# Layer 0's modulation, split between the preamble's TensorE and VectorE inside the latent-attention heads

## The chip, the cores and the metric

The kernel runs on one NeuronCore of a Trainium2 chip. The metric is the device time of one execution in microseconds (us); the median of the runs is compared.

## The reference, cut to what matters

One step of a four-layer trunk over 128 context and 512 latent tokens, model width D = 1024, float32. Each layer is

```python
mod = (jax.nn.silu(cond) @ w_mod[l] + b_mod[l]).reshape(cond.shape[0], 6, D_MODEL)[:, :, None, :]
h = rmsnorm(x, g_norm1[l]) * (1.0 + mod[:, 1]) + mod[:, 0]
out, ctx_tensors = token_mixer(l, h, ctx)
x = x + mod[:, 2] * out
h = rmsnorm(x, g_norm2[l]) * (1.0 + mod[:, 4]) + mod[:, 3]
x = x + mod[:, 5] * swiglu(h, w_ffn_in[l], w_ffn_out[l])
```

`cond` is one vector for the context tokens and another for the latent ones, so the modulation of a layer is a product of two rows of 1024 with a matrix of 1024 x 6144 (24 MB): six kinds of 1024 values, for two conditions. Kinds 0 and 1 (shift and scale) are used at the start of a layer, kind 2 after its token mixer, kinds 3 to 5 in its feed-forward part. The token mixer of layer 0 is latent attention with 8 heads.

## The kernel before, in words

The activations lie transposed in SBUF, 128 channels to a tile, 640 tokens to a row. Every large product is made of float32r multiplies of a high and a low part: a weight panel is fetched into `raw`, split into `w_hi` and `w_lo`, and TensorE multiplies three combinations (L310). The five engines have a program each, joined by semaphores; the order on each is written out by hand.

**Preamble.** The input is turned into tiles by TensorE (L829) and copied by ScalarE (L1342, L1343). VectorE sums the squares (L1862, L1864). Small vectors are turned into `vecs`, from which ScalarE makes `silu_c`, the 2 x 1024 activated conditions. Then `first_modulation` works out all six kinds of layer 0's modulation: 12 chunks of 512 columns, each fetched in one DMA of 2 MB (L649, L654) and multiplied by 8 TensorE multiplies with `silu_c` as the two-column weight (L761). ScalarE copies each two-row result (L1374) and TensorE turns it into columns, four small multiplies a chunk (L768). VectorE adds the bias (L1932). Only then come the first norm (column sums L326, the factor on ScalarE, `scaled` on VectorE L2009, the modulation of each tile on ScalarE L1389 and L1392, the low part L2014) and the projection into the latent ranks (`mla_in`, 6 panels).

**Layers 1 to 3** have their modulation worked out on VectorE, inside the previous layer's feed-forward part: a tile of `w_mod` is multiplied by a column of `silu_c` and added to an accumulator (L1971, L1973), and TensorE turns and VectorE sums the accumulators.

**A latent-attention head.** While TensorE multiplies for head h, it prepares head n = h + 1. Its order is: `gqn(n)`, scores 2, turned 0, `gqr(n)`, `ssqn(n)`, scores 3, `ssqr(n)`, `gkn(n)`, turned 1, `rotqr(n)`, scores 4, `sskn(n)`, `gv(n)`, turned 2 to 4, scores 0 and 1 of head n, `turned_v(n)` among them, and last the output product `pe_output` (L373). Here "scores t" is a query tile against all keys (L354) and "turned t" the transposition of its probabilities (L365). VectorE's order is: maximum 2, probabilities 2, maximum 3, `q_nope`, `q_rope` (L451), `q_roped` (L455, L456, L458), maximum 4, probabilities 3, `k_nope`, probabilities 4, then maxima 0 and 1 of head n, probabilities 0, `split_head` (L467 to L472), probabilities 1. ScalarE makes the exponentials (L388), the norm factors (L412, L414) and the copies. GpSimd splits the panels of the heads (L731 `w_hi`, L734 `w_lo`), one pair of operations when `gqr` is done and one when `gv` is done. The queue SP fetches each head's two panels as soon as `raw` is free; behind the last head's panels stand those of the output projection `wo0`, which ScalarE and VectorE split (`first_low_parts`). The last head prepares nothing and is shorter.

Of the kernel before, what the change touches and what calls it, by code (L numbers as in the profile page):

```python
# [18 lines left out]
ALU = mybir.AluOpType  # L19
# [3 lines left out]
P = 128  # L23
D = 1024
# [149 lines left out]
def build(nc, a):  # L174
# [3 lines left out]
    with ExitStack() as ctx:  # L178
# [57 lines left out]
        mod_ready = sem("mod_ready")  # L236
        mod_turned = sem("mod_turned")
        mod_summed = sem("mod_summed")
        scratch_free = sem("scratch_free")
# [19 lines left out]
        PRE = [Steps(pre_pe, ["x0", "x1", "x2", "x3", "x4", "x5", "x6", "x7", "vecs", "bmod", "lam"]),  # L259
               Steps(pre_act, ["vecs", "silu", "lamexp", "sp"]),  # L260
               Steps(pre_dve, ["ready", "lamsum", "lamdiff", "lamall", "bmod", "splog"])]
# [290 lines left out]
        first_mod_w = [work[:, k * KT * 512:(k + 1) * KT * 512] for k in (2, 1, 0)]  # L552
        first_mod_rows = work[0:2, WORK - 2 * 512:WORK].rearrange("p (b n) -> p b n", b=2)
# [26 lines left out]
        def _(sp):  # L580
# [64 lines left out]
            w = a["w_mod"][0].rearrange("(k p) n -> p k n", p=P)  # L645
            for b in range(3):
                if b == 1:
                    sp.wait_ge(scratch_free, 1)
                sp.dma_start(first_mod_w[b].rearrange("p (k n) -> p k n", k=KT),  # L649
                             w[:, :, b * 512:(b + 1) * 512]).then_inc(first_mod_in[b], 16)  # L650
            with sp.Fori(1, 4) as i:
                for b in range(3):
                    sp.wait_ge(first_mod_used, i * 3 + (b + 1 - 3))
                    sp.dma_start(first_mod_w[b].rearrange("p (k n) -> p k n", k=KT),  # L654
                                 w[:, :, bass.ds(i * 1536 + b * 512, 512)]).then_inc(first_mod_in[b], 16)

            for layer in range(DEPTH):
                if layer == 0:
                    win = a["mla_w_in"][0].rearrange("(k p) n -> p k n", p=P)
# [3 lines left out]
                    ph = phases["mla_in"]  # L663
                    for t in range(6):
                        c0 = t * P if t < 5 else 576
                        if t >= 2:
                            sp.wait_ge(split_done, t - 1)
                        sp.dma_start(raw[t % 2][:, :].rearrange("p (k n) -> p k n", k=KT),
                                     win[:, :, c0:c0 + P]).then_inc(raw_in[t % 2], 16)
                    panels("mla", lambda i, j: uq[:, :, bass.ds(i * 192, 192)] if j == 0  # L670
                           else ukv[:, :, bass.ds(i * 256, 256)])
# [81 lines left out]
        def _(pe):  # L753
            def first_modulation():

                with pe.Fori(0, 2) as i:
                    for q in range(7):
                        if q < 6:
                            pe.wait_ge(first_mod_in[q % 3], i * 32 + (16 * (q // 3) + 16))
                            for kt in range(KT):  # L760
                                last = nc.tensor.matmul(psum[q % 2][0:2, 0, :], silu_c[:, kt * 2:kt * 2 + 2],  # L761
                                                        first_mod_w[q % 3][:, kt * 512:(kt + 1) * 512],
                                                        start=(kt == 0), stop=(kt == KT - 1))
                            last.then_inc(first_mod_used, 1)
                        if q:
                            pe.wait_ge(first_mod_row, i * 6 + q)
                            for k in range(4):
                                last = nc.tensor.matmul(psC[:, 1, bass.ds(i * 48 + ((q - 1) * 4 + k) * 2, 2)],  # L768
                                                        first_mod_rows[:, (q - 1) % 2, k * P:(k + 1) * P],
                                                        ident[0:2, 0:2], start=True, stop=True)  # L770
                            last.then_inc(first_mod_turned, 1)
# [18 lines left out]
            LRU_PE.open(pe)  # L790

            def norm(n):
                if n == 0:
                    pe.wait_ge(mod_ready, 1)
                pe.wait_ge(square_done, (n + 1) * KT)
                sum_rows(psC, ones, [square_sum if n else square_sum0], TH).then_inc(sums_done, 1)
# [25 lines left out]
            pe.wait_ge(const_in, 16)  # L822
# [9 lines left out]
            pe.wait_ge(const_in, 16 * 22)  # L832
            for k in range(2):
                last = nc.tensor.transpose(psC[:, 0, k * P:(k + 1) * P], vec_rows[k], ident)
            pes.mark(last, "vecs")
            nc.tensor.transpose(psD[:, 0, 0:P], vec_rows[2], ident)
            pes.mark(nc.tensor.transpose(psD[:, 0, P:2 * P], vec_rows[3], ident), "bmod")
            dves.wait(pe, "lamdiff")
            pes.mark(nc.tensor.matmul(psC[:, 1, 0:1], ones[0:1, :], lam_tmp[0:1, 4:5], start=True, stop=True), "lam")
            acts.wait(pe, "silu")  # L840
            dves.wait(pe, "bmod")
            dves.wait(pe, "lamall")
# [3 lines left out]
            for layer in range(DEPTH):  # L846
# [6 lines left out]
                if layer == 0:  # L853
# [93 lines left out]
                    def head(h, more):  # L947
# [372 lines left out]
        def _(act):  # L1320
# [17 lines left out]
            act.dma_start(tables[:, :], a["tables"]).then_inc(tables_in, 16)  # L1338
# [13 lines left out]
            act.sem_inc(first_mod_turned, 2)  # L1352
            pes.wait(act, "vecs")
            act.sem_inc(silu_done, 1)
# [4 lines left out]
            acts.mark(nc.scalar.activation(sc[:, :, 1], vecs[:, VEC["c"]:VEC["c"] + KT], ACT.Silu), "silu")  # L1359
            dves.wait(act, "lamsum")  # L1360
            acts.mark(nc.scalar.activation(lam_tmp[0:1, 2:4], lam_tmp[0:1, 0:2], ACT.Exp), "lamexp")

# [4 lines left out]


            with act.Fori(0, 6) as i:
                for b in range(2):  # L1370
                    act.wait_ge(first_mod_used, i * 2 + (b + 1))

                    act.wait_ge(first_mod_turned, i * 2 + (b + 1))
                    nc.scalar.activation(first_mod_rows[:, b, :], psum[b][0:2, 0, :],  # L1374
                                         ACT.Copy).then_inc(first_mod_row, 1)
# [1070 lines left out]
```

## Time and profile before

| | us |
|---|---|
| median of 3 runs (3607.37 to 3613.88) | 3607.74 |
| the profiled execution | 3609.12 |
| its span, first to last instruction | 3606.8 |
| TensorE busy in the span | 3318.1 (92%) |
| VectorE busy | 1878.0 (52%) |
| ScalarE busy | 1132.7 (31%) |
| GpSimd busy | 117.5 (3%) |

The span is what the profiler saw between the first and the last instruction; 2.3 us of the execution lie around it. PE is TensorE's multiplying part, PEld its loading of weights, DVE VectorE, ACT ScalarE, POOL GpSimd, SP the queue that issues most DMAs. A share of busy time is an average over stages that differ; the mean granted TensorE clock of the whole span is 0.963 of full speed.

### The profile page before, as it was taken

The numbers are of one execution on the slowest core, as the hardware profiler recorded it, in microseconds if no ns is written. First come the engines' busy times: TensorE is split into PE (matmuls) and PEld (weight loads), VectorE is DVE, ScalarE is ACT, GpSimd is POOL, SyncE is SP. The second block draws the span as 40 slices with busy tenths as digits, with TensorE's granted clock in tenths as the row PEclk, the third lists the DMA queues.
The fourth block names the chain that finished last, engine by engine and source line by source line (L and its number), as shares of the span: only waits on it lengthen the run. The fifth ranks groups of instructions, "written<-read, shape, count | busy, mean of one in ns | idle before, by whom it ended". The sixth has DMA issues, their size and how long they took to land.

```text
span 3606.8 us, 52935 instructions
## 1 busy us (share of the span) xinstructions
PE 3318.1 (92%) x20320; PEld 3011.4 (83%) x20320; DVE 1878.0 (52%) x2728; ACT 1132.7 (31%) x1742; POOL 117.5 (3%) x72
## 2 busy tenths in 40 slices
PE   7979898999998998899999788989999897899999
PEld 2556677999987776789999766779999897899999
DVE  2133346858354666466763544567573688533333
ACT  1334433211125555232111333232111377321111
POOL 0311100000000000000000221000000000000000
PEclk9989999999999999899999899999999999999999
DMA  7300013444221110153532210143432221222222
GB/s 260 109 21 13 18 33 120 145 146 142 74 82 37 42 47 17 47 176 120 177 93 70 57 31 18 35 145 124 162 123 76 62 67 47 59 76 76 76 74 77
DMA packets 421861, 304.11 MB, mean 84 GB/s; under 512 B 12019, under 2 KB 389494, under 8 KB 421622
## 3 DMA queue, kind: packets, MB, share of 16 engines
q1 hardware_dynamic: 411412, 293.23, 26.2%
q10 hardware_dynamic: 10338, 9.41, 0.8%
q8 instruction: 69, 1.13, 0.1%
q14 instruction: 42, 0.34, 0.0%
HBM read 298.49 MB, written 4.10 MB: 84 GB/s over the span
## 4 chain that ended last, share of the span: by engine, by line
PE 83%; DVE 7%; ACT 5%; DVEq 2%; issue 2%; ACTq 1%; DMA 1%; SPq 0%
PE psB L310 29%; PE psA L310 29%; PE psD L310 7%; PE psC L373 3%; PE psA L354 2%; PE psC L326 2%; PE psC L365 2%; PE psB L354 2%; ACT h_hi L1392 1%; PE psA L761 1%; ACT work L1389 1%; PE psB L761 1%; ACTq L1391 1%; ACT work L412 1%; DMA raw<-in_w_ffn_in 1%
## 5 line engine op out<-in xcount | busy, mean ns | idle before, releaser
L1410 ACT ACTIVATE w_hi<-raw 128x1024 fp32r<-128x1024 f32 (+1 forms) x309 | 319.3, 1035 | 1165.2 <-PE psB L310 766.2
L1943 DVE TENSOR_TENSOR w_lo<-raw,w_hi 128x1024 fp32r<-128x1024 f32 (+1 forms) x309 | 367.9, 1192 | 347.8 <-ACT w_hi L1410 347.5
L310 PE MATMUL psA<-h_hi,w_hi 128*128 128x320 f32 x1616 | 384.5, 320 | 72.0 <-DVE h_lo L2014 59.9
L310 PE MATMUL psB<-h_hi,w_hi 128*128 128x320 f32 x1616 | 370.0, 310 | 15.5 <-DVE w_lo L2296 15.5
L310 PE MATMUL psA<-h_lo,w_hi 128*128 128x320 f32 x1616 | 375.4, 314 | 0.0
L310 PE MATMUL psA<-h_hi,w_lo 128*128 128x320 f32 x1616 | 375.1, 314 | 0.0
L310 PE MATMUL psB<-h_lo,w_hi 128*128 128x320 f32 x1616 | 369.2, 310 | 0.0
L310 PE MATMUL psB<-h_hi,w_lo 128*128 128x320 f32 x1616 | 369.1, 310 | 0.0
L310 PEld LDWEIGHTS psA<-h_hi,w_hi 128*128 128x128 f32 x1616 | 273.9, 192 | 91.9 <-issue 43.8
L1973 DVE SCALAR_TENSOR_TENSOR work<-work,silu_c 128x1024 f32<-128x1024 f32 x252 | 312.5, 1281 | 12.4 <-issue 0.9
L310 PEld LDWEIGHTS psB<-h_hi,w_hi 128*128 128x128 f32 x1616 | 271.0, 188 | 17.1 <-DVE w_lo L2296 17.1
L310 PEld LDWEIGHTS psA<-h_lo,w_hi 128*128 128x128 f32 x1616 | 277.2, 192 | 0.0
L310 PEld LDWEIGHTS psA<-h_hi,w_lo 128*128 128x128 f32 x1616 | 276.8, 192 | 0.0
L310 PEld LDWEIGHTS psB<-h_lo,w_hi 128*128 128x128 f32 x1616 | 271.3, 188 | 0.0
L310 PEld LDWEIGHTS psB<-h_hi,w_lo 128*128 128x128 f32 x1616 | 271.1, 188 | 0.0
L310 PE MATMUL psA<-act_hi,w_hi 128*128 128x320 f32 x960 | 221.5, 312 | 16.0 <-DVE w_lo L1943 14.9
L310 PE MATMUL psA<-act_lo,w_hi 128*128 128x320 f32 x960 | 220.3, 311 | 0.0
L310 PE MATMUL psA<-act_hi,w_lo 128*128 128x320 f32 x960 | 220.0, 311 | 0.0
L310 PE MATMUL psB<-act_hi,w_hi 128*128 128x320 f32 x960 | 218.8, 309 | 0.0
L310 PE MATMUL psB<-act_hi,w_lo 128*128 128x320 f32 x960 | 218.7, 309 | 0.0
L310 PE MATMUL psB<-act_lo,w_hi 128*128 128x320 f32 x960 | 218.7, 309 | 0.0
L310 PE MATMUL psD<-h_hi,w_hi 128*128 128x320 f32 (+1 forms) x672 | 182.0, 353 | 17.5 <-DVE h_lo L2014 8.6
(290 smaller groups left out, 5137.8 us busy)
## 6 DMA issues: line engine op xcount, KB each, us to landing
raw<-in_w_ffn_in SPq DMA_DIRECT2D x176, 512.0 KB, 3.9
work<-in_w_mod SPq DMA_DIRECT2D x144, 512.0 KB, 4.8
raw<-in_w_ffn_out SPq DMA_DIRECT2D x64, 512.0 KB, 3.9
work<-in_w_mod SPq DMA_DIRECT2D x12, 2048.0 KB, 7.9
raw<-in_w_ffn_out SPq DMA_DIRECT2D x32, 384.0 KB, 3.3
raw<-in_diff_w_in SPq DMA_DIRECT2D x24, 512.0 KB, 3.8
raw<-in_lru_w_in SPq DMA_DIRECT2D x16, 512.0 KB, 4.0
raw<-in_gqa_w_in SPq DMA_DIRECT2D x12, 512.0 KB, 3.8
```

The source lines that it names most:

```text
L310: last = nc.tensor.matmul(out[:, b, 0:half], w[slot][:, kt * cols + c0:kt * cols + c0 + P], r[:, o:o + half], start=(kt == 0 and p == 0), ...
L326: last = nc.tensor.matmul(out[:, b, 0:half], ones_, sq[:, b * half:(b + 1) * half], start=(k == 0), stop=(k == len(pieces) - 1))
L354: last = nc.tensor.matmul(s[:, b, 0:n], q[:, q0:q0 + P], k[:, k0:k0 + n], start=(m == 0), stop=(m == len(pairs[c]) - 1))
L365: last = nc.tensor.transpose(psC[:, k // 4, (k % 4) * P:(k % 4 + 1) * P], probs[(h.k % 2 * QT + t) % 2][0][:, k * P:(k + 1) * P], ident)
L373: nc.tensor.matmul(psC[:, 0, 0:NLAT], V[:, (k + 1) * P:(k + 2) * P], PT[:, k * NLAT:(k + 1) * NLAT], start=(k == 0), stop=(k == 4))
L412: nc.scalar.activation(halves(out, half), ps[:, :, 0:half], ACT.Ln, bias=eps, scale=1.0 / count)
L761: last = nc.tensor.matmul(psum[q % 2][0:2, 0, :], silu_c[:, kt * 2:kt * 2 + 2], first_mod_w[q % 3][:, kt * 512:(kt + 1) * 512], start=(kt ...
L1389: nc.scalar.activation(s_, s_, ACT.Identity, bias=mod_col(layer, 3 * which, kt, cond), scale=gains[:, cond * KT + kt:cond * KT + kt + 1])
L1391: act.drain()
L1410: nc.scalar.activation(w_hi[s][:, 0:n], raw[s][:, 0:n], ACT.Copy).then_inc(hi_done, 1)
L1943: nc.vector.tensor_tensor(w_lo[s_][:, 0:n], raw[s_][:, 0:n], w_hi[s_][:, 0:n].bitcast(F32), ALU.subtract).then_inc(split_done, 1)
L1973: last = nc.vector.scalar_tensor_tensor(acc[cond], w_, c_, acc[cond], ALU.mult, ALU.add)
```

## The change

- In the preamble `first_modulation` works out kinds 0 and 1 alone. It goes by tiles of 128 rows and 2048 columns (8 DMAs of 1 MB, three buffers), 4 multiplies a tile into two banks each of psA and psB: 32 multiplies in place of 96. Then come 2 copies on ScalarE and 16 turns on TensorE, in one go, in place of 12 copies and 48 turns in between. The first two `mla_in` panels are fetched behind the fourth and fifth tile.
- `silu_c` is made ahead of the copies of the input; the column sums of the first norm, its factor and `scaled` are made while the multiplies run; the small vectors of the last layer (`late_vectors`) are worked out behind the first norm.
- Kinds 2 to 5 (16 MB) are worked out in the 8 heads, 512 columns a head: 8 DMAs of 256 KB into two halves of `raw[2]`, 16 products on VectorE in four groups of 4 (`late(0)` to `late(3)`), into two accumulators that lie in the second half of `tables`, and 8 TensorE multiplies with one column of ones (`late_mod_turn`), behind turned 4.
- The second half of `tables` is fetched after the last head's `late_mod_turn`, in front of the panels of `wo0` on SP.

The diff, cut to its core:

```diff
             for kt in range(KT):
+                if kt >= 3:
+                    sp.wait_ge(first_mod_used, kt - 2)
+                sp.dma_start(first_mod_w[kt % 3], a["w_mod"][0][kt * P:(kt + 1) * P, 0:2 * D]).then_inc(first_mod_in[kt % 3], 16)
+                if kt in (3, 4):
+                    mla_in_panel(kt - 3)
...
+                    def late_mod(i, k):
+                        for kt in range(KT):
+                            sp.wait_ge(late_mod_used, i * (2 * KT) + (k * KT + kt + 1))
+                            sp.dma_start(late_mod_w[kt % 2], a["w_mod"][0][kt * P:(kt + 1) * P, bass.ds(i * D + (2 * D + k * 512), 512)]
+                                         ).then_inc(late_mod_in[kt % 2], 16)
...
+                    for k in range(2):
+                        late_mod(HEADS // 2 - 1, k)
+                    sp.wait_ge(late_mod_turned, HEADS + 1)
+                    sp.dma_start(tables[:, 2 * NLAT:4 * NLAT], a["tables"][:, 2 * NLAT:4 * NLAT]).then_inc(tables_in, 16)
...
+                for kt in range(KT):
+                    pe.wait_ge(first_mod_in[kt % 3], 16 * (kt // 3 + 1))
+                    for q in range(4):
+                        last = nc.tensor.matmul(psum[q // 2][0:2, q % 2, :], silu_c[:, kt * 2:kt * 2 + 2],
+                                                first_mod_w[kt % 3][:, q * 512:(q + 1) * 512],
+                                                start=(kt == 0), stop=(kt == KT - 1))
+                    last.then_inc(first_mod_used, 1)
...
+            def late_mod_turn(h):
+
+                pe.wait_ge(late_mod_used, h.at(KT, KT + 2))
+                for t in range(4):
+                    for cond in range(2):
+                        last = nc.tensor.matmul(psC[:, 1, bass.ds(h.at(8, late_at + t * 2 + cond), 1)],
+                                                late_mod_acc[cond][:, t * P:(t + 1) * P], ones[:, 0:1],
+                                                start=True, stop=True)
+                last.then_inc(late_mod_turned, 1)
...
                         pe_turned(pe, A, h, 4, m_probs)
+                        late_mod_turn(h)
                         if more:
...
+            def late_mod_product(h, n):
+
+                kt, cond = n // 2, n % 2
+                if cond == 0:
+                    if kt:
+                        dve.drain()
+                    dve.wait_ge(late_mod_in[kt % 2], h.at(64, 16 * (kt // 2 + 1)))
+                    if kt == 0:
+                        dve.wait_ge(late_mod_turned, h.at(1, 1))
+                w_, c_ = late_mod_w[kt % 2], silu_c[:, kt * 2 + cond:kt * 2 + cond + 1]
+                if kt == 0:
+                    last = nc.vector.tensor_scalar(late_mod_acc[cond], w_, c_, None, ALU.mult)
+                else:
+                    last = nc.vector.scalar_tensor_tensor(late_mod_acc[cond], w_, c_, late_mod_acc[cond], ALU.mult, ALU.add)
+                if cond:
+                    last.then_inc(late_mod_used, 1)
...
                         largest(h, 2)
                         probs(h, 2)
+                        late(0)
                         largest(h, 3)
                         prep(q_nope)
                         prep(q_rope)
+                        late(1)
                         prep(q_roped)
                         largest(h, 4)
                         probs(h, 3)
+                        late(2)
                         prep(k_nope)
                         probs(h, 4)
+                        late(3)
```

Three places where the order of instructions changes. First VectorE inside a head, from the probabilities of tile 2 (TENSOR_SCALAR 128x640) to `q_rope`. Before:

```order
L442 TENSOR_SCALAR work<-work 128x640
L95 REGISTER_ALU
L426 TENSOR_REDUCE work<-psB 128x1 [waits mla_att_pe]
L430 TENSOR_SCALAR work<-work 128x1
L95 ISA
L451 SCALAR_TENSOR_TENSOR work<-work,vecs 128x640 [waits mla_prep_act]
L95 REGISTER_ALU
L451 SCALAR_TENSOR_TENSOR work<-work,vecs 128x640 [waits mla_prep_act]
L95 ISA
L455 TENSOR_TENSOR work<-psC,tables 128x512 [waits mla_prep_pe]
```

And now, from the same TENSOR_SCALAR to `q_nope`:

```order
L444 TENSOR_SCALAR work<-work 128x640
L1991 ISA
L1993 ISA [waits late_mod_in0]
L1996 TENSOR_SCALAR tables<-raw,silu_c 128x512 [waits late_mod_turned]
L1996 TENSOR_SCALAR tables<-raw,silu_c 128x512
L1998 SCALAR_TENSOR_TENSOR tables<-raw,silu_c,tables 128x512 [waits late_mod_in1]
L1998 SCALAR_TENSOR_TENSOR tables<-raw,silu_c,tables 128x512
L95 REGISTER_ALU
L428 TENSOR_REDUCE work<-psB 128x1 [waits mla_att_pe]
L432 TENSOR_SCALAR work<-work 128x1
L95 ISA
L453 SCALAR_TENSOR_TENSOR work<-work,vecs 128x640 [waits mla_prep_act]
```

The four products of `late(0)` stand between the probabilities and the next maximum (TENSOR_REDUCE); the line numbers of the helpers are two higher. The other three groups stand in the same way ahead of `q_roped`, of `k_nope` and of the next head's first maximum.

Second TensorE at the end of a head, from turned 4 to the next head's scores 0. Before:

```order
L365 MATMUL psC<-consts,work 128x128 [waits mla_att_act,mla_att_dve]
L95 REGISTER_ALU
L354 MATMUL psB<-work 128x320 [waits mla_att_act,mla_prep_dve]
L354 MATMUL psB<-work 128x320 x3
L95 REGISTER_ALU [waits mla_att_act]
L934 MATMUL psC<-consts,work 128x128 [waits mla_prep_act]
L934 MATMUL psC<-consts,work 128x128 x5
```

And now, with the first and the last of the eight turns:

```order
L367 MATMUL psC<-consts,work 128x128 [waits mla_att_act,mla_att_dve]
L815 ISA [waits late_mod_used]
L815 MATMUL psC<-consts,tables 128x1
L815 ISA
...
L815 ISA
L815 MATMUL psC<-consts,tables 128x1
L95 REGISTER_ALU
L356 MATMUL psB<-work 128x320 [waits mla_att_act,mla_prep_dve]
L356 MATMUL psB<-work 128x320 x3
```

Eight multiplies of one column, behind a wait for VectorE's last product of the head, have come in between turned 4 and scores 0.

Third the queue SP from the heads to `wo0`. Before, the loop over the heads' panels and the first panel of `wo0` behind it:

```order
L595 ISA [waits split_done]
L595 DMA raw<-in_mla_w_uq 128x3x192
L594 REGISTER_ALU
L595 ISA [waits split_done]
L595 DMA raw<-in_mla_w_ukv 128x2x256
L607 REGISTER_ALU
L607 COMPARE_AND_BRANCH
L607 UNCONDITIONAL_BRANCH
L607 ISA
L595 ISA [waits split_done]
L595 DMA raw<-in_mla_w_o 128x8x128
```

And now, from the last two heads' tiles of `w_mod` on:

```order
L686 DMA raw<-in_w_mod 128x512 [waits late_mod_used] x16
L706 DMA tables<-in_tables 128x1024 [waits late_mod_turned]
L615 UNCONDITIONAL_BRANCH
L615 ISA
L603 ISA [waits split_done]
L603 DMA raw<-in_mla_w_o 128x8x128
```

The panels of `wo0` now stand behind a wait for the last head's turn and behind a fetch of 512 KB.

## Rows read from the trace of the kernel before

**Rows 1.** Stretches: us, busy PE, PEld, DVE, ACT, POOL; PEclk, DMA share, GB/s.

```profile
30.00:128.00 98.00, 97.39 (x288) 27.11 (x288) 4.77 (x31) 8.33 (x13) 8.43 (x4) 0.97 0.74 257
353.97:391.30 37.33, 32.90 (x152) 24.79 (x151) 13.93 (x31) 17.28 (x34) 4.87 (x4) 0.95 0.05 15
```

**Rows 2.** Chain of waits, preamble: start us, us, engine, tile, line, count.

```profile
30.48 9.47 PE psA L761 x16
39.95 6.87 PE psB L761 x16
46.82 0.98 PE psC L768 x8
...
127.92 0.33 DVE mods L1932 x2
...
132.16 0.49 ACT work L1389
```

**Rows 3.** Timeline of the start: start us, us, engine, line, operation [idle before].

```profile
12.49 0.60 ACT L1342 ACTIVATE x<-psA 128x512 f32<-128x512 f32 x1 [1.65 <-PE psA L829]
...
19.47 0.38 ACT L1355 ACTIVATE vecs<-psC 128x256 f32<-128x256 f32 x1
...
21.54 1.28 ACT L1361 ACT_TABLE_LOAD   x1
```

**Rows 4.** DMA issues of the first 200 us: count, KB each, us to landing.

```profile
work<-in_w_mod SPq DMA_DIRECT2D x12, 2048.0 KB, 7.9
raw<-in_mla_w_in SPq DMA_DIRECT2D x6, 512.0 KB, 3.9
...
raw<-in_mla_w_ukv SPq DMA_DIRECT2D x2, 256.0 KB, 2.7
```

**Rows 5.** Instructions that read silu_c: ns min/median/max, first and last start.

```profile
L1973 DVE SCALAR_TENSOR_TENSOR work<-work,silu_c x252: 1275/1282/1287, 609.8 to 2679.2; 128x1024 f32<-128x1024 f32 x126
```

**Rows 6.** Timeline of one head, 353.9 to 391.4 us.

```profile
355.82 0.55 DVE L442 TENSOR_SCALAR work<-work 128x640 f32<-128x640 f32 x1
...
356.69 1.15 POOL L731 TENSOR_TENSOR w_hi<-raw,consts 128x576 fp32r<-128x576 f32 x1 [15.47 <-PE psD L310]
...
359.87 0.82 DVE L426 TENSOR_REDUCE work<-psA 128x1 f32<-128x640 f32 x1 [3.50 <-PE psA L354]
...
362.58 0.89 DVE L451 SCALAR_TENSOR_TENSOR work<-work,vecs 128x640 f32<-128x640 f32 x1 [0.82 <-ACT work L414]
...
365.61 0.69 DVE L455 TENSOR_TENSOR work<-psC,tables 128x512 f32<-128x512 f32 x1 [2.15 <-PE psC L916]
...
367.72 1.56 PE L326 MATMUL psC<-work,consts 128*128 128x384 f32 x4 [1.70 <-DVE work L458]
...
373.53 0.29 DVE L442 TENSOR_SCALAR work<-work 128x128 f32<-128x128 f32 x1
...
375.68 0.41 PE L365 MATMUL psC<-consts,work 128*128 128x128 f32 x1
...
375.96 1.04 POOL L731 TENSOR_TENSOR w_hi<-raw,consts 128x512 fp32r<-128x512 f32 x1 [16.63 <-PE psD L310]
```

**Rows 7.** Timeline of VectorE beside GpSimd, 2010 to 2026 us.

```profile
2009.89 0.82 DVE L1862 TENSOR_TENSOR work<-x 128x640 f32 x1
...
2015.02 1.39 DVE L1862 TENSOR_TENSOR work<-x 128x640 f32<-128x640 f32 x1
...
2015.81 2.88 POOL L734 TENSOR_TENSOR w_lo<-raw,w_hi 128x1024 fp32r<-128x1024 f32 x1
...
2016.49 2.88 DVE L1864 TENSOR_TENSOR work<-work 128x640 f32<-128x640 f32 x1
```

**Rows 8.** Chain of waits at the end of the last head.

```profile
501.08 0.55 DVE work L442
...
506.83 6.06 PE psC L373 x10
...
513.10 7.04 PE psA L310 x48
```

More of the change, by code:

```diff
@@ L550, in build @@
         mod_acc = [[c(MUNIT) for _ in range(2)] for _ in range(2)]
-        first_mod_w = [work[:, k * KT * 512:(k + 1) * KT * 512] for k in (2, 1, 0)]
-        first_mod_rows = work[0:2, WORK - 2 * 512:WORK].rearrange("p (b n) -> p b n", b=2)
+        first_at = QT * D + 1024 + T
+        first_mod_w = [work[:, first_at + k * 2 * D:first_at + (k + 1) * 2 * D] for k in range(3)]
+        first_mod_rows = work[0:2, first_at:first_at + 2 * D]
+        first_rms = tables[:, 2 * NLAT:2 * NLAT + T]
+        late_mod_w = raw[2][:, 0:512], raw[2][:, 512:1024]
+        late_mod_acc = tables[:, 2 * NLAT:3 * NLAT], tables[:, 3 * NLAT:4 * NLAT]
+        late_at = 512 - 4 * 2 * KT
+        assert first_at + 6 * D <= WORK
         c = Carve()
@@ L662, in _ @@
                     wo = a["mla_w_o"][0]
[L663 to L671, printed above, removed]
+                    ph = phases["mla"]
@@ L754, in first_modulation @@
             def first_modulation():
[L756 to L771, printed above, removed]
+                for kt in range(KT):
+                    pe.wait_ge(first_mod_in[kt % 3], 16 * (kt // 3 + 1))
[4 more added lines that the diff above has]
+                    last.then_inc(first_mod_used, 1)
+                    if kt == 4:
+                        pe.wait_ge(square_done, KT)
+                        PRE[2].wait(pe, "lamdiff")
+                        sum_rows(psD, ones, [square_sum0], TH).then_inc(sums_done, 1)
+                        PRE[0].mark(nc.tensor.matmul(psC[:, 1, 0:1], ones[0:1, :], lam_tmp[0:1, 4:5], start=True, stop=True),
+                                    "lam")
@@ new lines, in first_modulation @@
+                pe.wait_ge(first_mod_row, 1)
+                for k in range(2 * KT):
+                    last = nc.tensor.matmul(psC[:, 0, 2 * k:2 * k + 2], first_mod_rows[:, k * P:(k + 1) * P],
+                                            ident[0:2, 0:2], start=True, stop=True)
+                last.then_inc(first_mod_turned, 1)
+            def late_mod_turn(h):
[6 more added lines that the diff above has]
+                last.then_inc(late_mod_turned, 1)
@@ L820, in _ @@
             pes, acts, dves = PRE
-            pe.wait_ge(const_in, 16)
+            pe.wait_ge(const_in, 16 * 22)
+            for k in range(2):
+                last = nc.tensor.transpose(psC[:, 0, k * P:(k + 1) * P], vec_rows[k], ident)
+            pes.mark(last, "vecs")
+            nc.tensor.transpose(psD[:, 0, 0:P], vec_rows[2], ident)
+            pes.mark(nc.tensor.transpose(psD[:, 0, P:2 * P], vec_rows[3], ident), "bmod")
             pe.wait_ge(x_in, 32)
@@ L831, in _ @@
                 pes.mark(last, f"x{kt}")
[L832 to L839, printed above, removed]
             acts.wait(pe, "silu")
-            dves.wait(pe, "bmod")
-            dves.wait(pe, "lamall")
             pe.wait_ge(x_done, KT)
@@ L1907, in _, with late_vectors @@
+            dve.drain()
+            def late_vectors():
+                dve.wait_ge(tables_in, 16)
+                acts.wait(dve, "sp")
+                ys, s_, s2, acc, tmp = (lru_small[:, 80 + 16 * k:96 + 16 * k] for k in range(5))
+                nc.vector.tensor_scalar(tmp, ys, 2.0, None, ALU.add)
                 dve.drain()
-                nc.vector.tensor_scalar(acc, acc, 1.0 / k, None, ALU.add)
+                nc.vector.reciprocal(tmp, tmp)
                 dve.drain()
-            nc.vector.tensor_tensor(acc, acc, s_, ALU.mult)
```

189 lines of the change are left out of this document (113 added, 76 removed).

## Prediction

> **What bounds the kernel now.** I read the table of stretches first. In the preamble TensorE is busy for 97.39 of 98.00 us, and with the modulation alone; a head takes 37.33 us, 32.90 of them TensorE's, while VectorE works 13.93 [rows 1]. The chain of waits says the same of the preamble: from 30.48 us it runs through L761 and L768 without a gap, until VectorE adds the bias at 127.92 and ScalarE modulates the first tile at 132.16 [rows 2]. What is taken from L761 there comes off the time one for one. A head is different. Its timeline shows a relay [rows 6]: TensorE turns, VectorE makes `q_roped`, TensorE's sums at 367.72 are released by VectorE after 1.70 us of waiting. VectorE has room on average, but a product in the wrong place lands on that relay. Last comes the end of the last head, where TensorE goes from L373 straight into `wo0` at 513.10 [rows 8].
>
> **Preamble: what goes.** Behind the landing of the small vectors, now turned first (about 11.7 us), ScalarE runs from the copy of `vecs` to the end of the second table load. Before, that was 19.47 to 22.82, so 3.35 us, and the eight input copies took 12.49 to 19.47, so 7.0 us [rows 3]. With 0.2 for the exponential that makes 11.7 + 3.4 + 0.2 + 7.0 = 22.3; 0.7 more as TensorE turns the tiles with idle time in between: 23.0. Eight multiplies took 6.87 us, the first eight 9.47 [rows 2]. So 32 take 27.5, and I add 1.3, half of the slow start (ends 0 and 2.6). The column sums of the norm, now among them, cost 1.1 by their columns, the small lambda multiply 0.3: end at 53.2. Then one after the other: two copies of 2 x 1024 by ScalarE, some 2.2 (estimate: a copy of 1024 columns, twice); 16 turns at 0.98 us for 4, so 3.9, and 0.8 for a TensorE that has just been idle (ends 0 and 3); VectorE's bias 0.33, gains and a flag, 1.1 in all. Sum 61.2, and 0.5 for hand-overs: ScalarE's first tile at 61.7 in place of 132.16, a gain of **70.4 us**, ends 66 and 73. Squares, column sums and `scaled` fit beside the multiplies: VectorE is done with them by about 52. The small vectors of the last layer, 31 operations of some 0.2 us, go behind the norm, where VectorE waits for the six panels anyway. DMA: 8 MB in 8 fetches, three of them issued from 9.5 us, when TensorE starts at 23; 2 MB landed after 7.9 us, 0.5 MB after 3.9 [rows 4], so 1 MB in about 5, and a buffer has 2 x 3.4 us. No wait, even with two panels in between.
>
> **A head with preparation (seven).** One product of 512 columns: the form of 1024 takes 1.28 us [rows 5], a two-input operation of 512 takes 0.69 (L455) [rows 6]; I take 0.74, a pair 1.4, a group of four 2.9, `late(0)` 2.4 as its first two have one tensor input.
> - `late(0)` starts at 356.4, behind the TENSOR_SCALAR of 355.82, and must be done by 359.87: hidden.
> - `late(1)` starts where `q_rope` ends, 363.5, and ends at 366.5; `q_roped` started at 365.61. **0.9 us** on the relay. TensorE's sums, and what hangs on them, come 0.9 later.
> - `late(2)` stands ahead of `k_nope`, which ends at 374.1; scores 0, which wait for it, were not due before 376. Hidden. Probabilities 4 then end at 374.8 (373.82 before), 0.9 later like the rest.
> - `late(3)` ends at 377.8. TensorE has done turned 4, at 376.1 + 0.9 = 377.0. It stands for **0.8 us**, and behind it on TensorE stand scores 0, `turned_v`, scores 1 and the output product.
> - 8 turns: L768 does 4 multiplies with as many loads in 0.98 us, so **2.1 us** with the hand-over.
> - The 64 fetches of 256 KB: one is issued when the product two tiles earlier is done and lands 2.7 us later [rows 4]. Tile 4 is asked for at 365.0, needed at 370.1; tile 6 at 371.6, needed at 374.9. They fit, the last by 0.6 us. On SP each head's panels stand ahead of its tiles and were waiting in `raw` before; nobody waits for them.
>
> That is 3.8 us, the floor, with two things to add that the trace of before shows in other places. Beside GpSimd a VectorE operation of two SBUF inputs and 640 columns, 0.82 us alone, took 1.39 and 2.88 [rows 7]. The second ends at 2019.37, 0.68 behind GpSimd's end at 2018.69: the two take turns. In a head GpSimd splits at 356.69 (2.6 us with its low part) and 375.96 [rows 6], inside `late(0)` and `late(3)`. If they take turns, `late(0)` ends near 361.2 and pushes `q_rope` by 0.6, `late(3)` by 1.1: 1.5 together, in the six heads with a split. I take 1.0, since a pair may pass without a break.
>
> Those rows bear out the Trainium skill, SBUF — State Buffer, section "SBUF: two separate sides": VectorE operations of two SBUF inputs and GpSimd operations exclude each other for a whole instruction. By that rule to the letter the heads cost 3 us more than with my 1.0 (6 x 0.5); without it, 6 us less. The trace agrees, in this one place.
>
> The other is the clock. A head's granted clock is 0.95 [rows 1], which is 3.7 us at half speed of 37.3, around 373.5 to 377 where TensorE waits between turns. The new stand and the one-column turns come right behind. More time at 1.2 GHz would fall on scores 0 and `turned_v`: I take 1.2 us a head, ends 0 and 3.
>
> So 3.8 + 1.0 + 1.2 = 6.0 for six heads and 5.0 for the seventh: **41.0 us**, ends 26.6 and 56.
>
> **The last head** has no other work to hide in. Its products and their fetches form a chain, since a tile lands 2.8 us after the product two tiles back. Probabilities 2 end at 501.6 [rows 8]; tiles 0 and 1 are done at 502.6 and 504.1; tiles 2 and 3 land at 505.4 and 506.9, done 506.8 and 508.4; maximum 4 and probabilities 3 take 1.4; tiles 4 and 5 land at 509.6 and 511.2, done 511.2 and 512.7; tiles 6 and 7 land at 514.0 and 515.5, the last is done at 517.0. The turns end at 519.1, and the output product starts there in place of 506.83 [rows 8]: 12.3 us. Then `wo0`: SP issues 512 KB of tables and two panels only at 519.1; the first panel lands near 524.4, ScalarE and VectorE split it in 2.4: TensorE starts at 526.8 in place of 513.10. **13.7 us**, and 0.8 for the clock: 14.5, ends 12 and 17.
>
> **Sum.** -70.4 + 41.0 + 14.5 = -14.9. On the profiled execution's 3609.1 that gives 3594.2. It lies 1.4 above the median of the runs, so 3592.8 on the median; I put down **3593**. A difference of 0.2% is 7.2 us, about what a measurement can tell.
>
> **Rivals.**
> - *Cheap heads.* GpSimd and VectorE pass each other and the clock stays: heads 27, last head 13.7, so -70.4 + 40.3 = -30.1: 3578. For it: VectorE would still be busy only 25 of 41 us. Against: rows 7. Chance 0.17.
> - *The tiles land late.* The last tile of a group has 0.6 us to spare. If a fetch takes 3.9 as one of 512 KB does, `late(3)` ends 0.6 to 1.2 later in each of seven heads and the last head's chain grows by 3: +9 us, 3602, no change that can be told. Also here: a preamble bound by its landings (+5). Chance 0.16.
> - *Half clock (slower).* Place: TensorE between turned 4 and the output product. It stands, loads weights for single columns, and is granted 1.2 GHz for turns, scores 0, `turned_v` and scores 1, 7.1 us of work at full speed with the turns; less what was slow already (0.6), some 6 us a head in place of 1.2. Seven heads: +34 us, 3626. For it: the clock fell at smaller gaps (0.95). Against: scores are dense work, behind which it rose each time. It decides from 7.9 us a head on ((70.4 - 14.5) / 7); slower by 0.2% needs 9.0. Chance 0.13.
> - *The change doesn't do what it says:* the preamble stays bound by something else, such as the copies of the input; the timeline leaves nothing that long. Chance 0.02, at 3600 or more.
>
> **How the numbers follow.** My forecast has 0.52, from 3584 to 3600. Faster by over 0.2% (under 3600.5): nearly all of that, the cheap heads, and little of the late tiles: 0.69. Same: part of the late tiles and the milder half of the slow clock: 0.19. Slower: 0.12. The range leaves out the ends of the cheap heads and the upper half of the slow clock: 3574 to 3616.
>
> **What would show it.** L761 with 32 multiplies ending near 53 us and the first L1389 near 62. A head of 43.3 us, of which TensorE waits about 1 to 2 behind VectorE's last product; `q_roped` released by the products, not by TensorE; VectorE products of over 1 us beside GpSimd; L815 at some 2 us a head. `wo0` starting 14 us after its old distance from the last head's first score, released by a DMA. I am wrong if a head takes under 41 or over 45 us, if tiles of `w_mod` release VectorE in the middle heads, or if the first norm comes after 66.

## The result, and the profile after

The changed kernel takes **3624.07 us** (median of 5 runs, 3618.60 to 3629.20); the kernel before 3607.74. The ratio is **1.0046**, 95% interval 1.0032 to 1.0059: slower, by 16 us, where 15 us less were forecast. The profiled execution took 3624.07 us, its span is 3621.7 us (before 3606.8). The page's first lines, of after:

```profile
PE 3302.8 (91%) x20256; PEld 3032.7 (84%) x20256; DVE 1991.5 (55%) x2858; ACT 1125.7 (31%) x1731; POOL 121.6 (3%) x72
...
PEclk9888889999998999999999899999999999999999
```

**The preamble did what was forecast.** Its chain of waits (start, us, what):

```profile
26.21 1.88 PE psA L794 x4
28.09 1.72 PE psB L794 x4
...
53.80 1.73 PE psB L794 x4
...
57.52 4.38 PE psC L806 x32
...
62.76 0.49 ACT work L1434
```

The multiplies end at 55.53 us, the turns at 61.9, ScalarE's first tile of the norm starts at 62.76; before, it was 132.16 [rows 2]. That is 69.4 us gained.

**The heads gave it all back.** The stretch of one regular head of after (the columns are those of [rows 1]):

```profile
314.80:362.55 47.75, 39.66 (x167) 29.80 (x167) 27.89 (x47) 17.27 (x34) 5.62 (x4) 0.86 0.18 56
```

A head takes 47.75 us, before 37.33 [rows 1]; the granted clock in it fell from 0.95 to 0.86. TensorE is *busier* (39.66 for 32.90) although only eight one-column multiplies came in: the same work lasts longer. The timeline shows where. L1998 is VectorE's late products, L815 the turns, L356 the scores, L766 and L769 GpSimd's splits of a panel, L328 the column sums, L977 `turned_v`:

```profile
329.40 2.31 PE L328 MATMUL psC<-work,consts 128*128 128x384 f32 x4 [2.53 <-DVE work L460]
...
330.94 2.92 DVE L1998 SCALAR_TENSOR_TENSOR tables<-raw,silu_c,tables 128x512 f32<-128x512 f32 x4 [0.16 <-issue]
...
336.41 4.53 DVE L1998 SCALAR_TENSOR_TENSOR tables<-raw,silu_c,tables 128x512 f32<-128x512 f32 x4 [0.17 <-issue]
...
337.30 1.42 POOL L766 TENSOR_TENSOR w_hi<-raw,consts 128x512 fp32r<-128x512 f32 x1 [17.09 <-PE psD L312]
...
338.80 1.59 POOL L769 TENSOR_TENSOR w_lo<-raw,w_hi 128x512 fp32r<-128x512 f32 x1
...
341.08 3.57 PE L815 MATMUL psC<-consts,tables 128*128 128x1 f32 x16 [3.68 <-DVE tables L1998]
344.51 4.62 PE L356 MATMUL psA<-work 128*128 128x320 f32 x8
348.92 1.49 PE L977 MATMUL psC<-consts,work 128*128 128x128 f32 x6
```

Read it from the back. Scores of 8 multiplies take 4.62 us here; the same form takes 2.32 in the dense parts of the head. The turns take 3.57. Ahead of them TensorE stood for 3.68 us, released by VectorE's last group of four products, which took 4.53 us in place of the 2.92 of the group before it: GpSimd's two splits lie inside it. The table of stretches has the granted clock: half (1.2 GHz) from 341.5 to 350, full (2.4 GHz) before TensorE stood:

```profile
335.00:337.00 2.00, 1.61 (x11) 1.00 0.67 176
341.50:350.00 8.50, 8.50 (x29) 0.50 0.28 93
```

From the last head's column sums (L328, 472.68) to the first multiply of `wo0` (529.69) it takes 57.0 us; before, 33.25 (479.61 to 512.86; the chain takes `wo0` up a little later [rows 8]). 7.9 of these 23.8 us lie ahead of the seventh head's output product. The chain of waits shows the other 15.9: tiles of `w_mod` that land one by one, the turns at half clock, and only then the fetch of `wo0`'s first panel:

```profile
513.46 2.53 DMA raw<-in_w_mod
...
516.03 1.43 DVE tables L1998 x2
...
517.50 3.59 PE psC L815 x16
...
521.77 5.38 DMA raw<-in_mla_w_o
...
527.17 1.06 ACT w_hi L1455
...
528.33 1.24 DVE w_lo L2007
...
529.69 1.43 PE psA L312 x8
```

So `wo0` starts 16.8 us late: -69.4 in the preamble, +15.9 at the last head's end, and +70.3 in the seven heads between, 10.0 each. The spans differ by 14.9, so nothing behind it adds to the loss.

### The profile page after: what moved, and what is told of

It reads as the page before. It is cut to its first block, busy times and chain, and to the rows that moved or that the text cites. A ratio compares the mean times of both kernels' runs of the same rounds, so it can differ in the third digit from the quotient of the medians.

```text
span 3621.7 us, 53111 instructions
## 1 busy us (share of the span) xinstructions
PE 3302.8 (91%) x20256; PEld 3032.7 (84%) x20256; DVE 1991.5 (55%) x2858; ACT 1125.7 (31%) x1731; POOL 121.6 (3%) x72
## 4 chain that ended last, share of the span: by engine, by line
PE 81%; DVE 7%; ACT 5%; DVEq 2%; issue 2%; DMA 1%; ACTq 1%; SPq 0%
PE psB L312 29%; PE psA L312 29%; PE psD L312 7%; PE psC L375 3%; PE psA L356 3%; PE psC L328 2%; PE psB L356 2%; PE psC L367 1%; ACT h_hi L1437 1%; ACT work L1434 1%; DVE tables L1998 1%; ACTq L1436 1%; PE psC L815 1%; DMA raw<-in_w_ffn_in 1%; DVE work L460 1%
```

## The experiments

Theory: TensorE standing behind VectorE's last product costs twice, the wait itself and the half clock behind it. Rivals: VectorE's products on the relay; the one-column multiplies themselves; the traffic of 2 MB a head. Each kernel below is made from the changed one. "Head" is the mean distance from one head's column sums of 384 columns (L328) to the next head's, over the last six; "end" runs from the last of these sums to the first multiply of `wo0`. The whole of the change and of "turns moved", "both" and "both, bias parted" is the median of 5, 4, 6 and 4 runs. Every other kernel below the change was run once. They ran on three chips, on which the median of the kernel before was 3602.78 to 3607.39 us and its single runs lay between 3594.47 and 3611.71. A difference of less than some 10 us in such a whole tells nothing by itself; the arguments rest on the heads and ends, which are read from the profiles:

| kernel | us | head | end |
|---|---|---|---|
| before | 3607.74 | 37.1 | 33.3 |
| the change | 3624.07 | 47.3 | 57.0 |
| no late work | 3546.70 | 36.9 | 36.2 |
| products | 3560.55 | 37.7 | 46.1 |
| products and turns | 3578.42 | 39.7 | 52.2 |
| products and wait | 3597.35 | 44.0 | 50.7 |
| change, wait filled | 3611.74 | 44.4 | 59.4 |
| change, short splits | 3602.15 | 44.2 | 57.6 |
| change, turns moved | 3573.23 | 39.8 | 52.4 |
| change, end repaired | 3621.77 | 47.3 | 47.7 |
| both | 3567.60 | 39.3 | 42.3 |
| both, bias parted | 3565.96 | 39.8 | 42.8 |

### Four kernels that take the late work apart

**Nothing of it.** Edit (out go SyncE's fetches, VectorE's products and TensorE's wait and turns; only the flag stays, and one multiply of constants fills the columns of kinds 2 to 5):

```diff
-                            late_mod(i, k)
...
-                pe.wait_ge(late_mod_used, h.at(KT, KT + 2))
-                for t in range(4):
...
+                pe.sem_inc(late_mod_turned, 1)
...
-                            for number in range(4):
-                                late_mod_product(h, 4 * k + number)
+                            pass
```

> Leaves out kinds 2 to 5 of layer 0's modulation altogether: no fetches of their weights, no products, no wait and no turns in the heads; their columns are filled with one constant multiply. It is the floor of the heads. All theories: a head takes 37.3 us again (47.75 with the change), granted clock 0.95 in it, the whole 3624 - 7 x 10.4 - 14 for the last head's chain = about 3537. If a head stays over 39 us, something else than the late work (code, the new buffers, the flag to SyncE) costs the time.

Measured: 3546.7 us (before, on the same chip, 3603.95); heads of 36.1 to 37.4. The end takes 3 us more than before, since the tables of layer 1 are still fetched ahead of its panels, which I had left out. The whole lies 10 us over what I expected. About 4 of them are there at `wo0`'s first multiply; the other 6 lie behind it, where both kernels have the same instructions, and in this one run they stay open. The late work as a whole costs the change 77 us.

**The products alone.** As above, but with fetches and products. As TensorE's flag no longer says that the accumulators in `tables` are free, SyncE waits for the last product before it fetches the tables:

```diff
                     sp.wait_ge(late_mod_turned, HEADS + 1)
+                    sp.wait_ge(late_mod_used, HEADS * KT + 2)
...
-                pe.wait_ge(late_mod_used, h.at(KT, KT + 2))
-                for t in range(4):
...
+                pe.sem_inc(late_mod_turned, 1)
```

> Keeps the fetches and VectorE's products, leaves out TensorE's wait for them and the turns, so kinds 2 to 5 are filled with a constant. Theory 'wait and clock' (mine): the products alone cost what they delay q_roped, 0.9 us, so a head of 38.2 to 38.8 us, scores to output product 5.4 us and the granted clock 0.95. Rival 'VectorE beside GpSimd': products of 1.8 to 2.4 us beside the splits push q_rope and the scores, and a head is 41 to 44 us with no wait of TensorE for a product. Rival 'traffic': the 2 MB a head slow the other fetches, a head of over 41 us with TensorE behind DMA.

Measured: 3560.55 us, heads of 37.7. The relay is later, as its row shows, TensorE waits 2.55 us for `q_roped` where it waited 1.70 [rows 6]:

```profile
340.71 1.83 PE L328 MATMUL psC<-work,consts 128*128 128x384 f32 x4 [2.55 <-DVE work L460]
```

But most of these 0.85 us come back: behind the sums TensorE no longer waits for ScalarE. 16 products and 2 MB of fetches cost a head 0.7 us over the kernel without them (37.65 less 36.92). Both rivals that blame VectorE's load or the traffic fall; The longer end (46.1 us, without them 36.2) makes 10 of the 14 us over the kernel without late work.

**Products and the wait, no turns:**

```diff
                 pe.wait_ge(late_mod_used, h.at(KT, KT + 2))
-                for t in range(4):
...
+                pe.sem_inc(late_mod_turned, 1)
```

> Keeps fetches, products and TensorE's wait for the last product of the head, leaves out the eight one-column multiplies (kinds 2 to 5 filled with a constant). If the standing TensorE brings the half clock: head 44 us (47.75 less the turns' 3.6), scores to output product still about 8 us, granted clock 0.86. If the one-column multiplies bring it: wait of 3.3 us and the 0.9 of the relay, head 41.5 us, scores to output product 5.4 us, clock 0.94 or more.

Measured: 3597.35 us, heads of 43.0 to 44.5, on average 6.3 over the products alone. TensorE's rows of this kernel and the clock in them (second view, columns us, TensorE busy, granted clock, DMA share, GB/s):

```profile
330.52 4.60 PE L356 MATMUL psA<-work 128*128 128x320 f32 x8 [3.93 <-DVE tables L1994]
334.92 1.44 PE L973 MATMUL psC<-consts,work 128*128 128x128 f32 x6
```

```profile
330.60:336.00 5.40, 5.40 (x14) 0.50 0.45 146
```

There is no one-column multiply here, and the scores are at half clock all the same. The wait does it.

**Products and eight one-column multiplies of a constant, no wait** (SyncE waits for the last product here too):

```diff
-                pe.wait_ge(late_mod_used, h.at(KT, KT + 2))
...
-                                                late_mod_acc[cond][:, t * P:(t + 1) * P], ones[:, 0:1],
+                                                ones, ones[:, 0:1],
```

> Keeps fetches and products, and eight one-column multiplies of a constant at the turn's place, but TensorE does not wait for the last product (kinds 2 to 5 not turned). If the standing TensorE brings the half clock: turns 2.1 us, head 37.3 + 0.9 + 2.1 = 40.3 us, scores to output product 5.4 us. If the one-column multiplies bring it: turns 3.6 us, scores to output product 8 us, head 44.4 us, clock below 0.9.

Measured: 3578.42 us, heads of 39.2 to 40.0.

```profile
315.90 2.18 PE L815 MATMUL psC<-consts 128*128 128x1 f32 x16
317.95 2.40 PE L356 MATMUL psA<-work 128*128 128x320 f32 x8
```

The turns cost 2.2 us and the scores behind them 2.40. So a head is 37.7 with the products, 39.7 with turns, 44.0 with the wait, 47.3 with both. Apart, turns and wait cost 2.0 and 6.3, together 9.6. The rest, 1.3, is about what the turns themselves lose behind the wait: 3.57 us in place of 2.18.

### The wait without the standing

22 multiplies of a constant stand ahead of the wait, where TensorE would be idle:

```diff
+                for _ in range(22):
+                    nc.tensor.matmul(psC[:, 1, 0:P], ones, ones, start=True, stop=True)
                 pe.wait_ge(late_mod_used, h.at(KT, KT + 2))
```

> The change, with 22 multiplies of constants (128 columns each, about 3.3 us, their result is never read) on TensorE ahead of its wait for VectorE's last product: TensorE works where it stood, and then waits for the rest. It parts the wait itself from the half clock behind it. If what it stood for brought the half clock: turns 1.9 us in place of 3.6, scores 2.4 to 2.5 in place of 4.5, the wait as long as before in sum (multiplies and rest 3.7), head 47.7 - 1.7 - 2.1 - 0.5 = 43.5 us, whole 3624 - 7 x 4.3 = 3594, granted clock in the heads 0.95. Rival 'the one-column multiplies bring it, or the work behind a wait is slow for another reason': head 47.5 us, scores over 4 us, 3622.

```profile
329.73 5.08 PE L813 MATMUL psC<-consts 128*128 128x128 f32 x44
...
334.64 1.84 PE L817 MATMUL psC<-consts,tables 128*128 128x1 f32 x16
336.35 2.40 PE L356 MATMUL psA<-work 128*128 128x320 f32 x8
```

```profile
334.70:343.50 8.80, 8.80 (x44) 1.00 0.23 76
```

Useless work makes the heads shorter: 44.4 in place of 47.3, though the filling takes 4.9 us, 1.2 more than the wait did. `wo0`'s first multiply comes 15.4 us earlier than in the change (514.24, not 529.69). The whole is 3611.74 us, 12 less, in one run on a chip where the kernel before took 3602.78. The clock stays at its upper level, the turns take 1.84 us in place of 3.57, the scores 2.40 in place of 4.62. The half clock alone is worth 2.9 + 1.2 = 4.1 us a head; by the rows 4.6 (1.7 turns, 2.2 scores, 0.7 `turned_v`).

The whole missed the expected 3594 by 18 us. The 22 multiplies were put at 3.3 us and took 4.9, so that a head is 0.9 longer than expected. In the last head, where TensorE had waited just before, they took 6.99, so that the end is 2.4 us longer than the change's and not some 4 shorter. Some 6 us of the miss stay open.

### GpSimd out of the last group

```diff
                     n = ph.shape[j][0] * ph.shape[j][1]
+                    if name == "mla" and not peeled:
+                        n = 16
```

> The change with GpSimd's splits of the heads' panels cut to 16 columns each (the other columns of these panels are not split, so the heads' projections are computed from old data); the instructions, waits and flags are all there. Theory 'VectorE and GpSimd take turns': the pair group of 1.83 us beside the split and the last group of 4.53 us fall to 1.0 and 2.9 us, TensorE's wait from 3.7 to 2.1 us, and a head to 46.1 us if the clock still falls, to under 44 if a wait of 2.1 us no longer brings the half clock. Rival 'the last product is late for another reason (its fetch)': the group stays over 4 us and the head at 47.5.

Measured: 3602.15 us. TensorE's column sums, VectorE's last group, GpSimd beside it, and the turns:

```profile
318.99 1.56 PE L328 MATMUL psC<-work,consts 128*128 128x384 f32 x4 [2.56 <-DVE work L460]
...
325.25 2.92 DVE L2000 SCALAR_TENSOR_TENSOR tables<-raw,silu_c,tables 128x512 f32<-128x512 f32 x4 [0.17 <-issue]
...
326.13 0.61 POOL L768 TENSOR_TENSOR w_hi<-raw,consts 128x16 fp32r<-128x16 f32 x1 [18.46 <-PE psD L312]
...
328.32 3.26 PE L817 MATMUL psC<-consts,tables 128*128 128x1 f32 x16 [2.08 <-DVE tables L2000]
```

The group falls from 4.53 to 2.92 us and the wait from 3.68 to 2.08: the same 1.6. VectorE's products and GpSimd's splits do hold each other up. With the wait at 2.08 us the turns still take 3.26 and the next scores 4.40. Heads are 42.5 to 45.3, mean 44.2 (452.26 less 187.01, over six), lower than the 46.1 I expected: besides the wait's 1.6, the sums run at full clock again (1.56, not 2.31) and 1.3 us more come off between the turns and the next head's sums. What of that is GpSimd's other split, beside the first products, no run tells apart.

### The turns moved

```diff
                         pe_turned(pe, A, h, 4, m_probs)
-                        late_mod_turn(h)
                         if more:
                             scores(n, 0)
                             A[1].wait(pe, "pt4", h)
                             turned_v(n)
                             scores(n, 1)
                             acts.wait(pe, "v", n)
+                        late_mod_turn(h)
                         pe_output(pe, A, pv, h, mV[h.k % 2], m_PT, m_PTp)
```

> The whole computation, with one thing moved: the eight one-column multiplies of a head stand right ahead of the output product, behind the next head's first two scores and turned_v, instead of ahead of them. After the first four runs the theory is: what costs most is that TensorE stands behind VectorE's last product, and then works at half clock; 0.25 us a multiply is the turns' own price. By it TensorE finds the products done (they end 3.7 us after it stood, and 5 us of work now lie before), a head takes 40.0 us, granted clock 0.93 or more, and the whole 3624 - 7 x 7.7 = 3570, or 3583 by the run without the wait (3578) and 4 for the turns in the last head's chain; I take 3583. Rival 'turns slow down the next work wherever they stand': the output product (4.46 us) takes over 6 us and a head stays over 43 us, 3605 or more.

Measured: **3573.23 us** (3565.36 to 3574.64), ratio to the kernel before 0.9905, interval 0.9885 to 0.9925; heads of 39.5 to 40.0, where 40.0 was expected.

```profile
314.19 2.92 DVE L1998 SCALAR_TENSOR_TENSOR tables<-raw,silu_c,tables 128x512 f32<-128x512 f32 x4 [0.17 <-issue]
316.33 2.50 PE L356 MATMUL psA<-work 128*128 128x320 f32 x8
316.41 1.59 POOL L766 TENSOR_TENSOR w_hi<-raw,consts 128x512 fp32r<-128x512 f32 x1 [17.68 <-PE psD L312]
...
321.49 1.84 PE L815 MATMUL psC<-consts,tables 128*128 128x1 f32 x16
...
323.19 4.54 PE L375 MATMUL psC<-work 128*128 128x512 f32 x10
```

Not one multiply less than the change has, and 51 us less. No wait stands in front of the turns; they take 1.84 us and the output product 4.54, so they slow down nothing. And the last group is back at 2.92 us: here only its last 0.7 us lie beside GpSimd's split (316.41, while the group ends at 317.11), and it is the split that takes longer, 1.59 us for the 1.04 of before [rows 6]. The whole is 10 us under what I expected, as the sum by differences (3570) had it.

### The end of the last head

The repair: in the last head the last four tiles' products go behind the output split and `wo0`'s first low parts on VectorE, SyncE asks for `wo0`'s first two panels ahead of these tiles and for the tables behind all panels, TensorE turns behind `wo0`'s first two panels.

```diff
                         if more:
                             probs(n, 1)
+                        else:
+                            late(2)
+                            late(3)
...
                         for kt in range(KT):
+                            if last and kt == 4:
+                                panels("wo0", wo0_panel, only_first=True)
...
-                if mod:
+                if mod or between:
                     turn(0)
-                    mod_turn(*mod, 2)
-                with pe.Fori(1 if mod else 0, KT // 2) as i:
+                    between() if between else mod_turn(*mod, 2)
+                with pe.Fori(1 if mod or between else 0, KT // 2) as i:
```

`between` is `late_mod_turn` of the last head.

Together with the moved turns:

> The whole computation: the turns moved as in the run before, and the end of the last head repaired: there the products of the last four row tiles follow the head's output split and wo0's first low parts on VectorE, SyncE asks for wo0's first two panels ahead of the last four tiles and for the layer-1 tables behind all of wo0's panels, and TensorE turns the last columns behind wo0's first two panels. If the 16.6 us at the last head's end were its chain of tiles, turns and the tables' fetch, wo0 starts within 3 us of its old distance from the last head's first score, and the whole is 3583 - 13 = 3570, 1% under the kernel before. If instead the late products only move their delay into wo0's first additions (VectorE), it gains under 5: 3579.

Alone:

> The whole computation: the end of the last head repaired alone, the turns of the other heads left where the change puts them. If the two faults add up: 3624 - 13 = 3611, with the heads still at 47.5 us. It should lie as far under the change as the fully repaired kernel lies under the one with the turns moved alone.

Measured: both **3567.60 us** (3562.49 to 3575.34), ratio 0.9901, interval 0.9885 to 0.9916; alone 3621.77. The expectation of 13 us missed: by the medians it is worth 6 us with the turns moved and 2 alone, and neither is clear of the spread of the runs (3562.49 to 3575.34 against 3565.36 to 3574.64; one run against 3618.60 to 3629.20). `wo0` does start 10 us earlier after the last sums (42.3 us; 52.4 with the turns moved alone), but its stretch to the next norm's sums grows from 59.6 to 68.1. The timeline of the kernel with both shows what gave it back:

```profile
480.71 1.84 PE L825 MATMUL psC<-consts,tables 128*128 128x1 f32 x16
...
482.58 0.29 DVE L2447 TENSOR_TENSOR mods<-psC,bmod 128x32 f32<-128x32 f32 x2 [6.70 <-PE psC L825]
...
487.72 0.89 PE L312 MATMUL psA<-act_hi,w_hi 128*128 128x320 f32 x2 [5.17 <-DVE w_lo L2019]
```

VectorE waits 6.70 us ahead of the bias, as the last eight columns are turned behind two panels; every addition of `wo0` stands behind that bias, and TensorE then waits 5.17. Of the 8.5 us that the stretch grew by, 5.2 are this wait and 1.7 the turns, which now lie in it; the other 1.6 fall on the 48 multiplies behind the wait, 8.68 us in place of 7.04. The same fault again, one stage on: a small late result in front of a whole queue. So the bias was parted:

```diff
+                            late_bias(0, HEADS - 1)
                             late(2)
                             late(3)
...
+                    turn(0, lambda j: low_part(name, 1, j))
+                    late_bias(HEADS - 1, HEADS)
```

`late_bias(a, b)` adds the bias to the columns of heads a to b - 1.

> The whole computation, both repairs, and the bias in two parts: the columns of the first seven heads get theirs right behind the last head's output split, the last head's eight columns behind wo0's first two tiles. In the run before this one VectorE stood 6.7 us ahead of the bias, since the turns of the last columns come behind wo0's first two panels, and wo0's second two panels started 5 us late. If that was what the repair of the end lost, wo0's panels follow each other without the gap (wo0 to the norm's sums 62 us in place of 68) and the whole is 3567.6 - 5 = 3562. If the panels' fetches are what is late instead: no gain, 3567.

Measured: 3565.96 us (3564.55 to 3568.84), ratio 0.9902, interval 0.9885 to 0.9918. The stretch is 61.4 us again, as expected, but the whole can't be told from the run before. Between the two profiled executions the heads lost 3.4 us (last sums at 427.62, in the other at 424.24): they take 39.4 to 40.0 us here and 39.9 and 38.6 in turn there, with the same instructions in them. Why is open. Either kernel is 1% under the kernel before, and some 1.5% under the change.

## Why the prediction was wrong

- **Preamble:** right. -69.4 for -70.4. TensorE started its multiplies at 26.21, not 23.0, as the small vectors were there at 14.57, not 11.7; the multiplies and sums were 0.9 shorter than reckoned and the steps behind them 1.3.
- **Products on the relay:** right in place (0.85 us, forecast 0.9). The run with the products alone shows that most of this comes back by the head's end. And the tiles of `w_mod` were in time: from 230 to 470 us of the change no DMA released VectorE.
- **Turns:** 2.1 forecast, 1.84 at full clock. Right, as a price of their own.
- **VectorE and GpSimd taking turns:** right in kind, not in place. `late(0)` took 4.3 us for 2.4 (317.12 to 321.42) and pushed nothing, where I had 0.6 for `q_rope`: ScalarE released that. At the last group it was 1.6 us (4.53 less 2.92) where I had 1.1. (0.6 and 1.1 make 1.7, not the 1.5 that the prediction has.) The run with GpSimd cut to 16 columns shows it by itself. It agrees in kind with the rule that the prediction took from the Trainium skill, SBUF — State Buffer, section "SBUF: two separate sides": four products of two SBUF inputs took what four take alone, plus 1.6. That the two exclude each other for the whole of each instruction isn't shown, as GpSimd's two operations took 2.3 us in the kernel before (1.04 and 1.27). I shaded that rule down to 1.0 for a whole head; the 1.5 that I had worked out by it was nearer.
- **The wait behind `late(3)`:** this step failed first. The prediction had 0.8 us, and up to 1.1 for GpSimd. It was 3.7. Reckoned from the head's sums, VectorE started the group at 7.0 us and not 6.3, TensorE was done at 8.0 and not 8.4, and GpSimd took 1.6: 0.8 + 0.7 + 0.4 + 1.6 = 3.5. The 0.7 and the 0.4 are the clock's too. The column sums took 2.31 us and not 1.56; in the kernel with short splits, where they took 1.56, the group starts 6.26 behind them (318.99 to 325.25). The multiplies ahead of turned 4 ran at the upper level (0.52 us for two records, 0.84 before), so that TensorE stood sooner. Each part is small; they add up because the group and TensorE meet at that point with nothing between them. A difference of two times of some 8 us each was treated as if it were good to 0.1.
- **The clock:** the step that decided. "I take 1.2 us a head, ends 0 and 3"; the run with the filled wait puts it at 4.1 to 4.6, outside its own ends. The rival "half clock" described what came, place included, with 6 us a head; it had a chance of 0.13. What spoke against it, "scores are dense work, behind which it rose each time", was wrong for this place: the clock stays down through the turns, 4.62 us of scores and `turned_v`, 9 us in all. The row that should have weighed more was in hand: where TensorE stood for 1.7 us or less [rows 6], the clock was 0.66 on average from 373 to 378 us, with TensorE busy throughout (table of stretches of before, columns as above):

```profile
373.00:378.00 5.00, 5.00 (x19) 0.66 0.00 0
```

- **Last head:** 15.9 for 14.5, its chain as described: tiles landing one by one, turns, fetch of `wo0`'s panel. The turns ran at half clock there too (3.59).
- **The sum:** the seven heads cost 70.3 for 41.0, the last head 1.4 more than forecast, the preamble gained 1.0 less: 31.7 in all; the time missed by 31.

In one sentence: the wait and the clock were costed as two small separate terms, but the first sets the second, and the two together, some 8 us, are four fifths of the 10 us that a head lost. That the clock would fall behind a wait was foreseen; its size, and how long the wait would be, were not.

## What to carry to other kernels

A wait on TensorE, where it sets the time, had two prices here: its own length, 3.7 us, and over 4 us for the slower clock of the dense work behind it. When a slack engine's result is needed by the bound engine, leave room for the errors of both timelines: consume it as late as the buffers allow, behind work that is ready, not at the first place where it is due. Moving eight multiplies down by three steps turned +0.5% into -1%. And look for every queue that the late result stands in front of: the wait for the last turn cost a fetch in SyncE's queue, then, once mended, a bias in VectorE's.

## What the runs showed of the hardware that I had not expected

- Standing for 2.08 us was followed by 7.6 us of unbroken work at a granted clock of 0.55, standing for 3.68 us by 8.5 us at 0.50.
- The length of a wait alone doesn't tell what follows: behind 2.53 to 2.56 us ahead of the column sums, these took 1.56 us with short splits, 1.83 with the products alone and 2.31 in the change. What decides between them no run shows.
- Eight one-column multiplies (sixteen records), with their weight loads, kept the clock where it was (0.97 over the 11 us around them) when TensorE had not stood, and ran at half speed when it had (3.57 for 1.84). They neither brought nor ended the low clock.
- Multiplies whose result nobody reads made a head 2.9 us shorter, by keeping TensorE busy through its wait, although they took 1.2 us more than the wait.
- 16 MB more of fetches beside the heads (60 to 76 GB/s between 200 and 430 us, where the kernel without late work moved 17 at most) cost them 0.7 us each, together with their products.
